# Two output pairs instead of one: seven block products for eight in a decoder layer's output projection

## The reference

```python
h = rmsnorm(x, norm_g)
z = h @ w_in
q_a, k_a, v_a, g_a, u_p, g_p, q_m, g_m = jnp.split(z, IN_OFFSETS, axis=-1)
y_a = moba_attention(q_a, k_a, v_a).reshape(B, S, MOBA_WIDTH) * jax.nn.silu(g_a)
y_p = multiscale_pool(u_p, w_pool, pool_scale) * jax.nn.silu(g_p)
mem_h = rmsnorm(mem, mem_norm_g)
mk, mv = jnp.split(mem_h @ w_mem_kv, 2, axis=-1)
y_m = memory_attention(q_m, mk, mv).reshape(B, S, MEM_WIDTH) * jax.nn.silu(g_m)
y = jnp.concatenate([y_a, y_p, y_m], axis=-1) @ w_out
return rmsnorm(x + y, final_norm_g)
```

## Time and profile before

| | us |
|---|---|
| median of 3 runs | 429.95 (429.71 to 430.3) |
| profiled execution, span from the first to the last instruction | 427.9 |
| TensorE busy | 419.0 |
| VectorE busy | 303.5 |
| ScalarE busy | 241.6 |
| GpSimd busy | 39.5 |

### The profile page before, as it was taken

One profiled execution on the slowest core, in us unless ns is written; L12 is line 12 of the kernel. 1 busy time (PEld: TensorE's weight loads), 2 busy tenths in 40 slices (PEclk: granted clock), 3 DMA queues, 4 the chain that ended last, 5 costly groups with the idle time before them and its releaser, 6 DMA issues.

```text
span 427.9 us, 5921 instructions
## 1 busy us (share of the span) xinstructions
PE 419.0 (98%) x2244; PEld 361.4 (84%) x2244; DVE 303.5 (71%) x330; ACT 241.6 (56%) x325; POOL 39.5 (9%) x64
## 2 busy tenths in 40 slices
PE   8999999999999999999999999999999999999993
PEld 7888888888888888888888888888899888888882
DVE  4875865456786699857466878877667488897842
ACT  6764784474363766464465446555565566765611
POOL 1000000000050000000000232302000201000160
PEclk9999999999999999999999999999999999999998
DMA  8999959998989528746336256465646999567023
GB/s 284 415 414 420 404 202 376 121 337 309 163 198 298 192 97 310 224 156 196 100 114 231 98 178 215 150 196 162 231 149 214 241 387 290 197 247 294 0 88 108
DMA packets 28251, 96.34 MB, mean 225 GB/s; under 512 B 3776, under 2 KB 4288, under 8 KB 27328
## 3 DMA queue, kind: packets, MB, share of 16 engines
q1 hardware_dynamic: 24624, 83.26, 57.4%
q0 software_dynamic: 1152, 4.19, 5.5%
q10 hardware_dynamic: 2448, 8.52, 5.5%
HBM read 93.87 MB, written 2.10 MB: 224 GB/s over the span
## 4 chain that ended last, share of the span: by engine, by line
PE 94%; issue 2%; DVE 1%; DMA 1%; DVEq 0%; POOLq 0%; POOL 0%; ACT 0%
PE ps L622 36%; PE ps L625 18%; PE ps L640 4%; PE ps L638 4%; PE ps L639 4%; PE ps L681 3%; PE ps L679 3%; PE ps L680 3%; PE ps L662 3%; PE ps L664 3%; PE ps L663 3%; PE ps L603 3%; PE ps L610 1%; DMA mem_raw<-in_mem_head 1%; PE ps L716 1%
## 5 line engine op out<-in xcount | busy, mean ns | idle before, releaser
L1098 DVE TENSOR_TENSOR w_lo<-w_raw,w_hi 128x1024 fp32r<-128x1024 f32 x133 | 165.7, 1262 | 72.9 <-ACT w_hi L863 72.4
L622 PE MATMUL ps<-xT,w_hi 128*128 128x512 f32 x640 | 201.9, 397 | 0.0
L863 ACT ACTIVATE w_hi<-w_raw 128x1024 fp32r<-128x1024 f32 x133 | 138.2, 1056 | 83.1 <-PE ps L625 49.5
L625 PEld LDWEIGHTS ps<-xT,w_lo 128*128 128x128 f32 x640 | 120.2, 188 | 28.4
L625 PE MATMUL ps<-xT,w_lo 128*128 128x256 f32 x640 | 125.8, 278 | 0.0
L622 PEld LDWEIGHTS ps<-xT,w_hi 128*128 128x128 f32 x640 | 97.8, 189 | 0.3
L975 ACT ACTIVATE part_b<-ps 128x1024 f32<-128x1024 f32 x11 | 11.3, 1026 | 18.2 <-PE ps L625 18.2
L639 PE MATMUL ps<-w_lo,yT 128*128 128x512 f32 x46 | 17.9, 389 | 0.0
L638 PE MATMUL ps<-w_hi,yT 128*128 128x512 f32 x46 | 17.9, 389 | 0.0
L640 PE MATMUL ps<-w_hi,yT 128*128 128x512 f32 x46 | 17.9, 389 | 0.0
L863 ACT ACTIVATE w_hi<-x_f 128x1024 fp32r<-128x1024 f32 x8 | 8.5, 1061 | 10.5 <-PE ps L681 5.1
(11 more groups left out here) (207 smaller groups left out, 622.1 us busy)
## 6 DMA issues: line engine op xcount, KB each, us to landing
w_raw<-in_w_in SPq DMA_DIRECT2D x94, 512.0 KB, 4.5
w_raw<-in_w_out SPq DMA_DIRECT2D x30, 512.0 KB, 5.2
w_raw<-in_w_mem_kv SPq DMA_DIRECT2D x13, 512.0 KB, 12.4
x_t_raw<-in_x_t SPq DMA_DIRECT2D x8, 256.0 KB, 13.1
rows<-in_x ACTq DMA_DIRECT2D x2, 1024.0 KB, 10.2
rows<-in_mem ACTq DMA_DIRECT2D x2, 1024.0 KB, 11.4
x_f<-in_w_in SPq DMA_DIRECT2D x4, 512.0 KB, 6.9
x_f<-in_w_in POOLq DMA_DIRECT2D x4, 512.0 KB, 11.1
```

What stands on the lines that cost most here:

```text
L622: pe.matmul(ps[:, bank0(g) + f, :], hi[:, t, f * P:(f + 1) * P], moving[:, kt], start=(kt == 0), stop=(kt == KT - 1), skip_group_check=True)
L625: m = pe.matmul(ps[:, bank0(g) + f, 0:S], lo[:, t, f * P:(f + 1) * P], moving[:, kt, 0], start=False, stop=(kt == KT - 1), skip_group_chec ...
L863: act.activation(halves_of(n)[0], whole_of(n), ACT.Copy).then_inc(hi_done, 1)
L1098: dve.tensor_tensor(lo, whole_of(n), hi.bitcast(F32), ALU.subtract).then_inc(lo_done, 1)
```

## The change

OUT0 with OUT1 and OUT2 with LAST become pairs; no output group is plain any more. The order of the units within a pair is new. The sums N5 and M4 of the output pairs are GpSimd additions of a loaded block and a piece in a slot; M1 and N7 stay VectorE additions, at other steps. GM's last steps move into the first pair. The x_res loads move behind the loop over the groups, and VectorE's wait for them ahead of the loop over the pairs. The split of the sums of `yT` blocks moves from OUT0 to GM. The extra buffers for LAST's splits are gone, and the end is rearranged: products and squares of the last two groups, and the order of GpSimd's products with the final gain. The V pair stays as it was. The diff, cut:

```diff
+def output_units(one, two):
+    return ((M2, 0), (M2, 1), (N5, 0), (N5, 1), (M3, 0), (one, 4), (M6, 0), (M1, 0), (one, 5), (M6, 1), (M1, 1),
+            (M3, 1), (one, 6))
+
+
+def output_loads(one, two):
+    return ((M2, 0), (M2, 1), (M6, 0), (M6, 1), (M3, 0), (one, 4), (M3, 1), (one, 5), (one, 6))
+
+
+PAIRS = ((V0, V1), (OUT0, OUT1), (OUT2, LAST))
+V_UNITS, V_LOADS = values_units(V0, V1), values_loads(V0, V1)
+OUT_UNITS = (output_units(OUT0, OUT1) + ((M4, 0), (M4, 1), (OUT0, 7), (OUT1, 4), (N7, 0), (OUT1, 5), (OUT1, 6),
+                                         (N7, 1), (OUT1, 7)),
+             output_units(OUT2, LAST) + ((LAST, 4), (LAST, 5), (OUT2, 7), (LAST, 6), (LAST, 7), (M4, 0), (M4, 1),
+                                         (N7, 0), (N7, 1)))
+LOADS = (tuple((1, g, a) for g, a in output_loads(OUT0, OUT1) + ((OUT0, 7), (OUT1, 4), (OUT1, 5), (OUT1, 6), (OUT1, 7)))
...
+POOL_SUMS = ((N5, 0), (N5, 1), (M4, 0), (M4, 1))
+DVE_SUMS = ((M1, 0), (M1, 1), (N7, 0), (N7, 1))
+DVE_SUM_STEPS = (1, 3, 7, 9)
+SUMS_AHEAD = 2
...
+BANK = {V0: 0, V1: 2, OUT0: 4, OUT1: 6, OUT2: 0, LAST: 2}
+LAST_PLAIN, LAST_N7, LAST_HALF = 4, 5, 6
...
+            for r, (q, g, a) in enumerate(LOADS):
+                if r == RAW:
                     sp.wait_ge(probs_turned, 2 * len(JOBS))
                     for i in range(BLOCKS):
-                        sp.dma_start(f4[:, i], out_w_dram[OUT2 - OUT0, 2 * i]).then_inc(f4_landed[1][i], 16)
-                if r == 5:
-                    sp.wait_ge(piece_used, OUT0 * PPG + EXTRA)
+                        sp.dma_start(f5_a[:, i], out_w_dram[0, 2 * i]).then_inc(f5_landed[0][i], 16)
+                if r == RAW + 2:
+                    sp.wait_ge(piece_used, PAIR)
                     for i in range(BLOCKS):
-                        sp.dma_start(f567[:, i, 0], out_w_dram[OUT1 - OUT0, 2 * i]).then_inc(f5_landed[1][i], 16)
+                        sp.dma_start(f5_b[:, i], out_w_dram[OUT2 - OUT0, 2 * i]).then_inc(f5_landed[1][i], 16)
                 if r < RAW:
-                    sp.wait_ge(lo_done, OUT0 * PPG + EXTRA + r + 1)
+                    sp.wait_ge(lo_done, PAIR - PPG + r + 1)
                 else:
-                    slot_free(1, *LOADS[r - RAW])
-                pair_load(1, OUT_PIECE + r, out_w_dram, OUT0, g, a)
+                    output_slot_free(*LOADS[r - RAW])
...
+            def output_sum(q, g, i):
+
+                f5 = f5_of(q)
+                if g == N5:
+                    pool.wait_ge(f5_landed[q - 1][i], 16)
+                    b12 = piece_landed(q, M2, i)
+                    if q == 1:
+                        pool.wait_ge(pv_done, 2 * len(JOBS))
+                    else:
+                        pool.wait_ge(lo_done, unit_in(1, N5, i) + 1)
+                        pool.wait_ge(f67_summed, output_sums_done(1, M1, i))
+                    out, left, right = f4[:, i], f5[:, i], b12
+                else:
+                    b21 = piece_landed(q, M6, i)
+                    pool.wait_ge(f_summed, output_sums_done(q, N5, i))
+                    out, left, right = f5[:, i], f5[:, i], b21
+                pool.tensor_tensor(out, left, right, ALU.add).then_inc(f_summed, 1)
...
-                    for k in range(BLOCKS):
-                        pool.wait_ge(f4_landed[1][k], 16)
-                        pool.dma_start(f4[:, k], out_w_dram[OUT1 - OUT0, 2 * k], accum_op=ALU.add
-                                       ).then_inc(f4_summed[1][k], 16)
+                    for f in POOL_SUMS[:SUMS_AHEAD]:
+                        output_sum(1, *f)
                 pool.wait_ge(gate_tanh, i + 1)
                 pool.wait_ge(att_ready, 2 * (i + 1))
...
+            for f in POOL_SUMS[SUMS_AHEAD:]:
+                output_sum(1, *f)
+            for f in POOL_SUMS:
+                output_sum(2, *f)
+
+            def weigh(g, h, squared_by):
+
+                c = slice((g - OUT0) * COLS, (g - OUT0 + 1) * COLS)
+                pool.wait_ge(sq_done, squared_by)
+                pool.tensor_tensor(x_res[:, h, c], x_res[:, h, c], fg[:, c], ALU.mult).then_inc(weighted, 1)
+
             pool.wait_ge(fg_landed, 16)
-            pool.wait_ge(lo_done, UNITS)
-            for g in range(OUT0, LAST):
-                c = (g - OUT0) * COLS
-                pool.wait_ge(sq_done, TH * (g - OUT0 + 1))
-                for h in range(TH):
-                    pool.tensor_tensor(x_res[:, h, c:c + COLS], x_res[:, h, c:c + COLS], fg[:, c:c + COLS],
-                                       ALU.mult).then_inc(weighted, 1)
+            for h in range(TH):
+                for g in (OUT0, OUT1):
+                    weigh(g, h, 4)
+            weigh(OUT2, 0, 5)
+            weigh(OUT2, 1, 7)
             for h in range(TH):
                 pool.wait_ge(ms2_ready, h + 1)
...
+            pe.wait_ge(att_ready, 2 * len(BRANCHES))
+            pe.wait_ge(y_lo, BLOCKS)
+            for n in range(PAIR, UNITS):
+                if n == PAIR_B:
+                    pe.wait_ge(evacuated, OUT0)
                 unit_of_pair(n)
...
-                if g == OUT0 and a == 0:
-                    act.wait_ge(pv_done, 6)
-                    for h in range(TH):
-                        act.dma_start(x_res[:, h], x_dram[h]).then_inc(res_landed, 16)
...
+            act.wait_ge(pv_done, 2 * len(JOBS))
+            for h in range(TH):
+                act.dma_start(x_res[:, h], x_dram[h]).then_inc(res_landed, 16)
             for n in range(PAIR, UNITS):
...
+                elif n >= PAIR:
+                    act.wait_ge(summed_by(g), output_sums_done(pair_of(n), g, i))
...
+            act.wait_ge(summed, 4)
+            square_sum(0, end, 3)
+            act.wait_ge(summed, 5)
+            square_sum(1, columns_of(OUT2), 2)
+
+            def scale_end(h):
...
+            scale_end(0)
+            for i, part in enumerate(LAST_PARTS):
+                act.wait_ge(summed, 6 + i)
+                square_sum(1, slice(end.start + part.start, end.start + part.stop), 3 + i)
+            scale_end(1)
...
+            def output_sum(q, g, i):
+
+                p = OUT_PIECE + LOADS.index((q, M6 if g == M1 else M3, i))
+                dve.wait_ge(landed[p % RAW], 16 * (p // RAW + 1))
+                if g == M1:
+                    dve.wait_ge(f_summed, output_sums_done(q, N5, i))
+                    dve.wait_ge(piece_used, PAIR)
+                    out, left = f6[:, i], f4[:, i]
+                else:
+                    dve.wait_ge(f67_summed, output_sums_done(q, M1, i))
+                    out, left = f7[:, i], f6[:, i]
+                dve.tensor_tensor(out, left, slot(p), ALU.add).then_inc(f67_summed, 1)
...
+            last_gate = len(GATES) - 1
+            dve.wait_ge(res_landed, 16 * TH)
             for n in range(PAIR, UNITS):
...
+                if n - BEGIN[pair_of(n)] in DVE_SUM_STEPS:
+                    output_sum(pair_of(n), *DVE_SUMS[DVE_SUM_STEPS.index(n - BEGIN[pair_of(n)])])
                 if n == PAIR + 5:
-                    combine(1, OUT1, 1, ALU.add)
-                if n == PAIR + 6:
-                    combine(0, OUT2, 0, ALU.add)
+                    dve.wait_ge(gate_att, last_gate + 1)
+                    dve.scalar_tensor_tensor(out=gate[:, :, :], in0=part_b[:, :, :], scalar=1.0, in1=gate[:, :, :],
+                                             op0=ALU.add, op1=ALU.mult).then_inc(y_ready, 1)
+                if n == PAIR + 7:
+                    dve.wait_ge(y_hi, last_gate + 1)
+                    dve.tensor_tensor(yT[:, NF * last_gate:, 1], gate[:, :, :], yT[:, NF * last_gate:, 0].bitcast(F32),
+                                      ALU.subtract).then_inc(y_lo, 1)
+                if n == PAIR + 8:
+                    combine(1, 0, OUT1, 0, ALU.add)
+                if n == PAIR + 9:
+                    combine(1, 1, OUT0, 1, ALU.add)
...
+            dve.wait_ge(piece_used, unit_in(2, LAST, 7) + 1)
+            add_last(0, bank0(LAST), end).then_inc(summed, 1)
+            settle(add_last(1, LAST_PLAIN, end))
+            dve.wait_ge(fg_landed, 16)
+            dve.wait_ge(summed, 4)
+            weigh_last(0, whole).then_inc(end_weighted, 1)
+            mean_of(0, 6)
+            dve.wait_ge(piece_used, unit_in(2, M4, 1) + 1)
+            add_last(1, bank0(LAST) + 1, before_end, ALU.subtract).then_inc(summed, 1)
+            settle(add_last(1, bank0(LAST) + 1, end))
+            finish(0, 5)
+            dve.wait_ge(half_used, 1)
+            add_last(1, LAST_N7, end).then_inc(summed, 1)
+            dve.wait_ge(summed, 6)
+            weigh_last(1, first)
+            dve.wait_ge(half_used, 2)
+            add_last(1, LAST_HALF, slice(end.start + second.start, end.stop)).then_inc(summed, 1)
+            dve.wait_ge(summed, 7)
+            weigh_last(1, second).then_inc(end_weighted, 1)
+            mean_of(1, 9)
+            finish(1, 6)
```

(40 more changed lines are left out.)

362 lines of the change are left out of this document (177 added, 185 removed).

## The result

The changed kernel takes 453.77 us (median of 4 runs, 451.87 to 454.02) against 430.12 beside it (four runs: 429.71 to 430.3 and one of 708.41): ratio 1.0539, interval 1.0511 to 1.0567. Forecast were 454.0. The profiled execution spans 451.9 us, 24.0 more than the 427.9 of before.

What follows compares the result with a forecast made beforehand. TensorE's matmul stream, busy 98% of the span, was taken as the bound. Terms: -2.7 + 3.0 + 7.1 + 2.9 + 5.0 + 4.8 + 4.0 = +24.1; with 427.9 and 2.1 this gives 454.0 us, range 441 to 461.

Steps and rivals of the forecast that it cites:

- Saving: Second output pair: 12 matmuls fewer at 0.227 us each, 2.72 us less TensorE work.
- A: Hand-over from GM to the first pair: TensorE idles 1.95, then 1.04 before unit 3; together 3.0 us.
- B: Ahead of unit 4: VectorE's early wait for x_res holds later splits; TensorE idle 7.07 us (bounds 5 and 12).
- Rival 2: GpSimd's sums don't hold VectorE up and x_res lands before VectorE wants it: 438.8 us, down to 435; chance 0.10.
- rival 4: Output stage: queues hide all forecast delays, both x_res loads landed by 342.9; 427.2 us, chance 0.05.
- C: First pair from unit 4: VectorE catches up on splits and sums; TensorE idle 2.9 us by unit 14 (bounds 1 and 4).
- side sentence: After the long gap units 4 and 5 run slow, some 2 us, mostly in idle time before unit 12: +24.6.
- rival 3: The clock stays low over units 4 to 12: +13, up to 467 us; chance 0.08.
- D: Second pair's four GpSimd sums, 2.40 each, delay VectorE's splits of units 17 to 19: 5.0 us idle (bounds 0 and 6).
- Rival 1: GpSimd's sums slip into VectorE's pauses and don't hold it up: +14.0, 444 us; chance 0.15.
- E: Second pair's first units: four GpSimd x_res gain products, 1.33 each, between VectorE's operations; 4.8 us reach TensorE (bounds 0 and 6).
- F: Kernel's end: final scaling begins 6.2 us after TensorE's end instead of 2.1; 4.0 more, 2.8 if VectorE is early.

Runs made afterwards that it cites:

- e6: Changed kernel with both copies of the attention result ahead of the split of N5 on ScalarE: 452.09 us.
- e9: Kernel before, with only VectorE's wait for the x_res loads moved to the first step behind GM: 436.02 us.
- e11: Changed kernel with only the second pair's four N5 and M4 sums made by VectorE instead of GpSimd: 448.44 us.
- e8: Changed kernel with constant matmuls (24, 11 and 8, no part of the result) put into three of TensorE's gaps: 450.03 us.
- e4: Changed kernel with the first four GpSimd gain products delayed until 16 units of the second pair are split: 449.77 us.
- e1: Changed kernel with VectorE's wait for the x_res loads moved to the first addition that needs them (step 8): 451.12 us.
- e5: Changed kernel with GpSimd's power for the first half of the tokens ahead of its product for OUT2's second half: 451.95 us.

## Why the prediction was right

**Saving.** Right: 12 matmuls, at 0.227 still the commonest distance, 2.7 us.

**A, the hand-over.** The first gap is 2.1 by the starts (1.95 forecast), through the chain named: sum, split, copies. The second gap, before unit 3, hardly exists: TensorE's clock had fallen, units 0 to 2 took longer, and the split of unit 3 (done at 342.9, as forecast) came in time. e6's trace shows what the sum had wrong: A doesn't add to B, it lies ahead of the same x_res. Its time is too spread to confirm that.

**B, the wait for x_res.** Mechanism and time are right: VectorE resumes at 349.75 (349.7 and 350.1 forecast). TensorE's gap is 5.8 by the starts and not 7.1, since slow units 0 to 2 brought TensorE there at 345.3 instead of 344.3. By itself the wait costs 5.6 (e9). Rival 2 (x_res lands in time) and rival 4 (faster) fall by VectorE's row of 6.84 idle us.

**C, catching up.** Mis-sized: 1.3 for 2.9 (1.0 before unit 12, 0.3 before unit 14). The units 4 and 5 ran at half clock until 356.3, some 2.5 us that VectorE used to catch up. The forecast's side sentence had this: by the Trainium skill's "TensorE: Matmul & The Clock Gate", part 1 (slow is the default, activity releases), units 4 and 5 would be slow and most of it would fall into this idle time. The trace agrees with it, 0.50 from 351.5 to 356 and 1.00 after it; rival 3, a clock that stays low, falls. What the sentence lacked is the other three spells.

**D, the second pair's sums.** Mechanism right, place wrong, idle time 2.8 for 5.0. That e11 gains 5.3 is no confirmation of the 5.0, since slow matmuls are in it. I had three gaps before units 17 to 19; there is one, 2.8 us before unit 21, with 3.4 us of half clock behind it. VectorE had split unit 17 by 376.7, where my count had it at 380.7: it was 4 us farther ahead than part C allowed. In e8's profiled execution, with fewer slow matmuls ahead of them, the three splits end at 380.8, 384.2 and 387.5, as counted (380.7, 384.2, 387.8), and the gaps lie before units 17 to 19. The 2.40 for each sum was too much for the changed kernel: VectorE lost 1.7 per sum. Rival 1 (no exclusion) falls by the rows of 2.88 and 3.42 and by e11.

**E, the gain products.** 0.6 for the snapshot and 1.9 in one gap instead of 4.8 idle, with a spell of half clock behind it; taken away the products give up to 4.0 (e4). They take 2.26 each and not 1.33, as they alternate with VectorE's operations, which lose some 4 us by it; only 1.9 of that reaches TensorE:

```profile
402.02 9.03 POOL L646 TENSOR_TENSOR x_res<-x_res,fg 128x512 f32<-128x512 f32 x4 [12.45 <-ACT squares L1010]
```

**F, the end.** Right in size and in order. On GpSimd, TensorE and VectorE, for the earlier trace rows:

```profile
440.75 1.26 POOL L646 TENSOR_TENSOR x_res<-x_res,fg 128x512 f32<-128x512 f32 x1 [5.00 <-ACT squares L1010]
441.98 0.57 POOL L656 TENSOR_TENSOR rstd<-ms,power 128x1 f32<-128x1 f32 x1
...
440.21 0.28 PE L774 MATMUL ps<-w_hi,yT 128*128 128x256 f32 x1
...
442.64 1.15 DVE L1554 TENSOR_SCALAR x_res<-x_res,rstd 128x512 f32<-128x512 f32 x2 [2.12 <-issue]
443.70 0.68 DVE L1536 TENSOR_TENSOR x_res<-x_res,ps 128x512 f32<-128x512 f32 x1
...
446.58 1.15 DVE L1554 TENSOR_SCALAR x_res<-x_res,rstd 128x512 f32<-128x512 f32 x2 [0.68 <-POOL rstd L656]
```

The product, the power behind it, the two scalings, and only then the last addition: from the last matmul's end (440.49) to the final scaling 6.1 us (6.2 forecast, 2.1 before).

**The sum.** It came out within 0.3 us of the median though idle time was forecast at 22.8 and is about 15. That is in good part luck. What isn't luck: VectorE is the engine that is late, so a slow TensorE spends some time in which it would otherwise have waited. The luck: e1 and e8 gain 2.7 and 3.7 with a higher clock, and of the changed kernel's own runs the one at 451.87 has a mean clock of 0.981 where the others, 453.75 to 454.02, have 0.973. So some 2 to 4 of the 6.2 us, an estimate from these differences, are a cost of its own that the sum had not. It stands in for idle time that C, D and E had too high.

Two signs of the forecast did not come: TensorE is busy 7.1 us longer and not 2.7 less, and it idles some 15 us in the stage and not over 20. Both come from the slow spells and from the sizes of C, D and E.

## What to carry over

A saving on the busiest engine counts only if the engines that feed it have room at the very steps where the new work is put: here VectorE had 6 us of 41 free, and a sum moved to GpSimd took 1.7 to 2.2 us of VectorE's time where VectorE itself needs 1.14. A wait on an in-order engine is priced by what is queued behind it, not by its own need; one moved wait cost 5.6 us in a kernel otherwise unchanged. And gaps of TensorE can cost twice, once as idle time and once as matmuls at half clock behind them (not every gap had such a spell), so a few long gaps, many short ones and filled ones have different prices for the same idle time.

## What was unexpected of the hardware

- The granted clock fell after or near the end of gaps as short as 2.1, 2.8 and 1.9 us (336 to 338, 388 to 390.7, 408 to 410), and was back after 3.4 us each time; at the 5.8 us gap it took 6.8, 1.6 of them inside the gap. But e4 and e11 have the same 2.1 us gap at the hand-over and no fall right behind it (their first spell begins at 348.4 and 346.4, inside the long gap that follows). What decides this was not found.
- When GpSimd and VectorE both have work queued, the turns aren't always alternate. The sum begun at 375.29 takes 4.81 while VectorE's operations at 375.50 and 376.64 run at their plain 1.22; only the third (378.31) is held up. The Trainium skill, "SBUF — State Buffer", "SBUF: two separate sides", says that whichever starts first has the shared ports for its whole instruction and the other is blocked. The lengthened operations agree with it (1.7 us of extra time per sum); the two at 375.50 and 376.64 don't, if the starts in the rows are taken as they stand. Who is served first when several are queued, that section doesn't say, and no run here settles it.
- Not every VectorE operation is held up by GpSimd. The addition at 387.44 takes one input from PSUM and runs at its plain 1.23 beside the sum of 386.75 to 389.57; its counterpart does so in e1, e4, e5 and e6 as well. The rule of the forecast, that the two engines exclude each other, is too wide: the operations that were lengthened here have all their inputs in SBUF.
